# Embedding products between the experts, and expert results added two token tiles at a time

## The reference

```python
x = x + merged @ w_o[i]
x = x + hierarchical_moe(rmsnorm(x, g_ffn[i]), ..., w_exp_gate[i], w_exp_up[i], w_exp_down[i])
ple_gate = jax.nn.sigmoid(rmsnorm(x, g_ple[i]) @ w_ple_gate[i])
x = x + (p[i] @ w_ple[i]) * ple_gate
```

## Time and profile before

| | us |
|---|---|
| three timed runs, median | 2404.42 |
| profiled execution | 2404.93 |
| its span in the trace | 2403.1 |
| TensorE busy in the span | 2284.4 (95%) |
| first add of layer 0 / of layer 1 (start of the embedding block) | 691.18 / 1432.98 |
| half 0 done, ScalarE's table load behind it, layer 0 / layer 1 | 729.56 / 1472.62 |

### The profile page before, as it was taken

The page is one execution under the profiler, slowest core; times in us unless marked ns, Lnnn a source line. Parts: engine busy times, 40 slices in busy tenths (PEclk is TensorE's granted clock), DMA queues, the critical chain, the costliest instruction groups (busy, mean ns, idle before and its releaser), DMA issues. The chain is left out here.

```text
span 2403.1 us, 29859 instructions
## 1 busy us (share of the span) xinstructions
PE 2284.4 (95%) x11904; PEld 1698.6 (71%) x11904; DVE 1003.0 (42%) x1787; ACT 597.2 (25%) x1245; POOL 415.3 (17%) x407
## 2 busy tenths in 40 slices
PE   9989999997899989999998888999989999999998
PEld 7666788654458767788754447877768887888887
DVE  6545533511146454543521136445643435232234
ACT  3523401311134442410311115323540003000012
POOL 2011111122212101111122211111102211111111
PEclk9999999999999999999999999999999999999999
DMA  5114536799962212234899982422213332333321
GB/s 170 46 52 107 134 106 256 319 421 423 420 246 70 62 38 71 58 98 167 327 420 422 422 335 74 108 80 84 81 38 101 91 120 72 103 97 97 97 97 71
DMA packets 291931, 396.57 MB, mean 165 GB/s; under 512 B 32591, under 2 KB 232015, under 8 KB 274379
## 3 DMA queue, kind: packets, MB, share of 16 engines
q1 hardware_dynamic: 274880, 366.27, 42.6%
q0 software_dynamic: 11328, 16.81, 1.9%
q10 hardware_dynamic: 5578, 11.51, 1.8%
HBM read 388.98 MB, written 30.15 MB: 174 GB/s over the span
## 5 line engine op out<-in xcount | busy, mean ns | idle before, releaser
L146 PE MATMUL banks<-h_split,w_high 128*128 128x512 f32 (+1 forms) x2640 | 827.0, 395 | 2.8 <-PEq L3450 1.7
L146 PEld LDWEIGHTS banks<-h_split,w_high 128*128 128x128 f32 x2640 | 482.8, 188 | 104.0 <-issue 8.2
L198 DVE TENSOR_TENSOR w_low<-w_raw,w_high 128x1024 fp32r<-128x1024 f32 (+1 forms) x264 | 321.8, 1220 | 503.3 <-POOL w_high L187 503.1
L187 POOL CAST w_high<-w_raw 128x1024 fp32r<-128x1024 f32 (+1 forms) x264 | 279.1, 1058 | 1434.8 <-PE banks L146 1312.0
L146 PE MATMUL banks<-h_split,w_low 128*128 128x512 f32 (+1 forms) x1320 | 513.5, 389 | 0.0
L146 PEld LDWEIGHTS banks<-h_split,w_low 128*128 128x128 f32 x1320 | 247.8, 188 | 52.4
L146 PE MATMUL banks<-w_high,op_split 128*128 128x512 f32 x736 | 228.5, 390 | 1.4 <-DVE mg_part L1425 1.1
L2159 PE MATMUL banks<-expert_ring,ex_xsT 128*64 128x256 f32 x1408 | 172.5, 401 | 35.2 <-DMA expert_ring<-in_w_exp_up 33.7
L2159 PEld LDWEIGHTS banks<-expert_ring,ex_xsT 128*64 128x64 f32 x1408 | 103.2, 144 | 92.4 <-DMA expert_ring<-in_w_exp_up 37.0
L146 PEld LDWEIGHTS banks<-w_high,op_split 128*128 128x128 f32 x736 | 138.1, 188 | 31.8 <-DVE mg_part L1425 2.4
L146 PE MATMUL banks<-w_low,op_split 128*128 128x512 f32 x368 | 143.2, 389 | 0.0
(11 more groups left out here) (446 smaller groups left out, 2745.6 us busy)
## 6 DMA issues: line engine op xcount, KB each, us to landing
w_raw<-in_w_in SPq DMA_DIRECT2D x142, 512.0 KB, 4.0
expert_ring<-in_w_exp_gate SPq DMA_DIRECT2D x42, 1024.0 KB, 20.6
expert_ring<-in_w_exp_up SPq DMA_DIRECT2D x42, 1024.0 KB, 23.9
expert_ring<-in_w_exp_down SPq DMA_DIRECT2D x42, 1024.0 KB, 23.5
region<-in_w_exp_gate SPq DMA_DIRECT2D x22, 1024.0 KB, 19.9
region<-in_w_exp_up SPq DMA_DIRECT2D x22, 1024.0 KB, 23.3
region<-in_w_exp_down SPq DMA_DIRECT2D x22, 1024.0 KB, 23.6
w_raw<-in_w_gu SPq DMA_DIRECT2D x44, 512.0 KB, 4.0
```

Of the source, the lines that this page charges most:

```text
L146: last = nc.tensor.matmul(out, left, right, start=(start and n == 0), stop=(stop and n == 2), skip_group_check=True)
L187: self.nc.gpsimd.tensor_copy(self.high[:, i % self.SPLIT, 0:n], self.raw[:, i % self.RAW, 0:n]).then_inc(self.high_ready, 1)
L198: self.nc.vector.tensor_tensor(self.low[:, i % self.SPLIT, 0:n], self.raw[:, i % self.RAW, 0:n], self.high[:, i % self.SPLIT, 0:n].bitcast ...
```

## The change

1. The embedding's eight half-tiles are multiplied on TensorE ahead of the experts at positions 16, 17 and 19 to 24 (BETWEEN), into PSUM bank 7, and ScalarE takes each ahead of that expert's silu. w_ple is loaded as one DMA of 1 MB behind the loads of expert 15, when position 11 has finished, into slot 5.
2. The slot of an expert comes from a table. From expert 12 on slot 5 is not used for experts any more, so five slots remain, and near the end three for the last loads.
3. The first four gate pieces wait for position 25 instead of 29. GpSimd and VectorE convert two of them ahead of the border (GATE_EARLY), the third behind it.
4. In the embedding block VectorE adds tiles 0 and 1 and one choice of tile 2, then forms the low parts of the first two tiles, then adds the rest. TensorE first issues 24 matmuls that nobody reads and 5 more behind each of the first three adds, then transposes the first two tiles, multiplies them by the first six chunks of half 0, and does the same for the other two tiles; the last two chunks follow for all four.
5. The norm's gain (norm_g, 4 KB) is loaded from ScalarE's queue instead of SyncE's.

```diff
-            for q in (e.pairs - 2, e.pairs - 1):
-                c = (q + 1) % GATHERS
-                sp.wait_ge(e.turned, 2 * q + 2)
-                sp.dma_start(*embedding.load_pair(c)).then_inc((p_landed0, p_landed1)[c], 16)
-            sp.wait_ge(e.down_done, EXPERTS - 2)
+                if n == SLOT_LEFT + 3:
+                    sp.wait_ge(e.down_done, SLOT_LEFT)
+                    embedding.load_weights(sp)
+            sp.wait_ge(e.down_done, e.order.index(GATE_RAW_AFTER) + 1)
             gate_stream.loads(sp, 0, gate_stream.RAW)
...
-            gate_stream.split_highs(pool, 0, gate_stream.SPLIT)
+            gate_stream.split_highs(pool, 0, GATE_EARLY)
...
+SLOT_OF = (*(n % 6 for n in range(17)), 0, 1, 2, 3, 4, 0, 1, 3, 4, 2, 0, 1, 3, 0, 1)
+SLOT_LEFT = 12
+GATE_RAW_AFTER, GATE_EARLY = 25, 2
-EARLY_PRODUCTS = 4
+BETWEEN = (16, 17, 19, 20, 21, 22, 23, 24)
...
+    def freed(self, sp, done, held):
+        if self.before(held):
+            sp.wait_ge(done, self.order.index(self.before(held)[-1]) + 1 if self.refilled else self.before(held)[-1] + 1)
...
     def tensor(pe):
-        for i in range(EARLY_PRODUCTS, 2 * NT):
-            wait(pe, embedding.ready, i - 1)
-            embedding.product(i, k.ps[:, i % 2, :]).then_inc(multiplied, 1)
-        for t in range(NT):
-            norm.open_tile(pe, t, (results.added, 2 * t + 2))
...
+        early = 2 * st.SPLIT
+        unread(k, 7, 24)
+        for n in (1, 2, 3):
+            pe.wait_ge(results.added, n)
+            unread(k, 7, 5)
+        for pair in range(PAIRS):
+            pe.wait_ge(results.added, 4 * pair + 4)
+            norm.turn_rows(pe, pair, k.x)
+            for c in range(early):
+                norm.pair_split(pe, pair, c)
+                st.rows(pe, c // 2, c % 2, 2, c, lambda t: k.ps[:, t, :], tiles=(2 * pair, 2 * pair + 1))
+        for c in range(early, DC):
+            norm.pair_split(pe, PAIRS - 1, c)
+            st.rows(pe, c // 2, c % 2, 2, c, lambda t: k.ps[:, t, :])
...
-        for t in range(NT):
+        for t in (0, 1):
             results.add(k, dve, gate, t)
+        dve.wait_ge(results.landed[2], 16)
+        results.add_choice(k, dve, gate, 2, 0)
         dve.wait_ge(norm.gain_landed, 16)
-        for step in "h0 h1 h2 h3 h4 w3 h5 h6 h7".split():
-            (norm.low if step[0] == "h" else st.split_low)(dve, int(step[1]))
+        for c in range(DC):
+            norm.low_pair(dve, 0, c)
+            if c == 3:
+                st.split_low(dve, 2)
+        results.add_choice(k, dve, gate, 2, 1)
+        results.add(k, dve, gate, 3)
+        for c in range(DC):
+            norm.low_pair(dve, 1, c)
+        st.split_low(dve, 3)
         norm.following_vector(dve)
```

More of the change, by code:

```diff
@@ L298, in scale @@
         self.nc.scalar.activation(x, x, ACT.Copy, scale=self.ss[:, t:t + 1]).then_inc(done, 1)
+PAIRS, PAIR = NT // 2, 2 * P
 class Norm:
+    places = tuple(tuple((bank + c // 2, c % 2 * PAIR) for c in range(DC)) for bank in (2, 4))
     def __init__(self, k, ctx, tag, gain, banks, xn, follows=False, small=None):
@@ L460, in turn_pair @@
     def turn_pair(self, pe, pair):
-        wait(pe, self.low_done, DC * pair)
         pe.wait_ge(self.xn_dve, pair + 1)
         pe.wait_ge(self.xn_act, pair + 1)
[L465 to L487, removed]
+        self.turn_rows(pe, pair, self.xn)
 class FinalNorm(LateNorm):
-    places = (LateNorm.places[0], tuple((5 + c // 2, c % 2 * PAIR) for c in range(6)) + ((0, PAIR), (1, PAIR)))
+    places = (Norm.places[0], tuple((5 + c // 2, c % 2 * PAIR) for c in range(6)) + ((0, PAIR), (1, PAIR)))
     def __init__(self, k, ctx, tag, gain, xn, junk, stream, closing, gained, g):
@@ L1741, in _ @@
             e.down(pe, 1)
[L1742 to L1745, removed]
-                wait(pe, embedding.ready, i - 1)
-                embedding.product(i, k.ps[:, i % 2, :]).then_inc(multiplied, 1)
+            e.multiply(pe, 2, embedding.product)
         @block.scalar
@@ L1791, in _ @@
             act.preload_act_table_set("silu_and_others")
[L1792 to L1795, removed]
+            e.activate(act, embedding.take)
         @block.vector
@@ L1973, in _ @@
             e.vectors(dve, 2)
-            for i in range(gate_stream.SPLIT):
+            for i in range(GATE_EARLY):
                 gate_stream.split_low(dve, i)
@@ L2061, in held, with slot, before @@
         return self.order[n] if self.order[n] < EXPERTS else RESIDENT
+    def slot(self, held):
+        return SLOT_OF[held] if self.refilled else held % len(self.slots)
+    def before(self, held):
+        return [n for n in range(held) if self.slot(n) == self.slot(held)]
+    def freed(self, sp, done, held):
+        if self.before(held):
+            sp.wait_ge(done, self.order.index(self.before(held)[-1]) + 1 if self.refilled else self.before(held)[-1] + 1)
     def refill(self, pool, out, weights, column, last_row, landed):
@@ L2171, in down @@
     def down(self, pe, n):
[L2172 to L2173 removed]
+        held = self.held(n)
+        u = self.slot(held)
+        pe.wait_ge(self.down_landed[u], 16 * (len(self.before(held)) + 1))
         if self.refilled and self.order[n] == EXPERTS:
@@ L2334, in tensor @@
     def tensor(pe):
-        for i in range(EARLY_PRODUCTS, 2 * NT):
-            wait(pe, embedding.ready, i - 1)
-            embedding.product(i, k.ps[:, i % 2, :]).then_inc(multiplied, 1)
-        for t in range(NT):
-            norm.open_tile(pe, t, (results.added, 2 * t + 2))
-        pe.wait_ge(embedding.ready, 2 * NT)
-        for e in range(pieces - st.SPLIT):
-            half = e // NT
-            for n in (0, 1):
-                c = 2 * (e % NT) + n
-                if half == 0:
-                    norm.turned_split(pe, c)
-                st.rows(pe, e, n, 2, c, lambda t: k.ps[:, half * NT + t, :])
-                if half == 0:
-                    norm.turn_next(pe, c)
+        early = 2 * st.SPLIT
[12 more added lines that the diff above has]
+            st.rows(pe, c // 2, c % 2, 2, c, lambda t: k.ps[:, t, :])
+        for e in range(NT, pieces - st.SPLIT):
+            for n in (0, 1):
+                st.rows(pe, e, n, 2, 2 * (e - NT) + n, lambda t: k.ps[:, NT + t, :])
         first = DC - 2 * st.SPLIT
```

114 lines of the change are left out of this document (70 added, 44 removed).

## The result

The kernel after takes 2411.63 us (median of 7 runs, 2408.85 to 2414.41) against 2403.89 us (7 runs) for the kernel before on the same chip: a ratio of 1.0031, 95% interval 1.0021 to 1.0040. It is slower, by 0.31%. The prediction (2399.6 us, 2394.5 to 2405.5) had the wrong sign, and the time lies outside its range. The profiled execution took 2409.78 us, span 2407.9, so its span is 4.8 us longer than the profiled one of before; by the medians the difference is 7.7 us. The traces can place the 4.8 us only.

A forecast was written before the change was run, and what follows sets the result against it. TensorE, busy 95% of the span, bounds the kernel, with experts paced by loads. Terms -0.1 + 0.3 (up to the first add) - 1.9 - 3.1 (to half 0's end) = -4.8 us, giving 2399.6 us, range 2394.5 to 2405.5.

The forecast's parts named there:

- w_ple among the loads: Expert stage: 1 MB in the saturated stream delays later expert loads, costing 2.1 us in layer 0, 2.5 in layer 1.
- The products: Between the experts: eight half-tiles, 14.3 us, hide in TensorE's 18.3 us of load waits; cost 0.
- the rival of a starved last expert: Expert stage: fewer slots make expert 31's loads land up to 8.5 us late per layer, 2416.6 us; chance 0.12.
- the prediction's sign for this rival: End of the experts: waits of several us for expert 30 or 31 would show starvation.
- The border: Last expert to first add: one cast and one conversion fewer bring the first add 2.2 us forward in each layer.
- the other reading: Conversions ahead of the first add: the 3.01 us one is long by itself, not from GpSimd overlap; gain only 1.2 us.
- To the end of half 0: Embedding block from the first add: takes 36.5 us, 1.9 us less in layer 0 and 3.1 less in layer 1.
- Later loads: Last gate piece and next block's loads issued some 4 us later, covered by conversions and sigmoids: 0, at most some 2 us.
- The clock: TensorE behind its idle at the border: 4 us at half clock, costing 2 us, falls on unread matmuls.
- the sum of -4.8 us: Whole kernel: net change -0.1 + 0.3 - 1.9 - 3.1 us against the profiled execution.

The follow-up runs named there:

- run 7: Kernel after, slot table kept, but w_ple loaded behind expert 31 and all eight half-tiles multiplied behind the last expert: 2434.80 us (one run).
- run 11: Kernel after, w_ple still loaded early, but all eight half-tiles multiplied behind the last expert: 2439.49 us (one run).
- run 9: Kernel after with all gate casts ahead of the next block's, piece 7's low part earlier and the next block's three spread out: 2405.53 us, ratio 1.0006.
- run 12: Kernel before with only the experts' part (early w_ple, slots, products between experts), embedding block as before: 2411.00 us, ratio 1.0036.

## Why the prediction was wrong

**w_ple among the loads** (+2.1 and +2.5): the mechanism held, the size did not: +3.2 and +3.3 (+3.2 and +3.0 by the means over the traces with and without the early load). The term took 1.049 MB at 421 GB/s, and the stream does run at that rate to about 640 us; behind that the rate fell. 640 to 672 us of before, and then of after (columns as in the earlier trace rows):

```profile
640.00:672.00 32.00, 30.50 (x225) 16.83 (x223) 5.55 (x15) 4.37 (x10) 9.05 (x9) 1.00 1.00 402
```

```profile
640.00:672.00 32.00, 30.45 (x225) 16.74 (x223) 5.38 (x14) 4.37 (x10) 9.04 (x9) 1.00 0.98 383
```

Whether that makes up the 0.5 to 0.8 us above 2.5 is not settled: run 7 has the low rate too (385 GB/s) and no delay.

**The products** (0) were hidden: run 11. **The slots**: the rival of a starved last expert did not come; its up load is issued at 659.46 instead of 649.80 and TensorE waits 2.3 us for it; but run 7, with the same table, waits even 2.9 us there and has no delay, so a wait at this place, the prediction's sign for this rival, does not show it.

**The border** (-2.2 each): VectorE's conversions end 2.1 us earlier against the last gate_up, as worked out. But the first add then waits for y_rows to land (2.3 us of idle where it was 1.8), so 1.6 and 1.4 are left. The two conversions took 3.17 us beside GpSimd's casts, more than twice 1.21; this is the overlap that the prediction took from its row, and the 2.1 us agree with it, where the other reading gave 1.2. It is also what the Trainium skill says (GPSIMD Engine Reference, Key points): the two engines share SBUF interfaces, and an instruction with two SBUF inputs contends.

**To the end of half 0** (-1.9 and -3.1): -2.0 and -2.9. The unread matmuls took 10.5 and 11.0 us against 10.9, and TensorE reached the first transposes well behind the fourth add, as the prediction said. That it fits to 0.2 us is in part luck: in the other five traces with 39 unread matmuls these took 9.2 to 12.1 us and this stretch of the table 37.0 to 39.0 us. The shortest (run 7, layer 0) had none of them at 1.2 GHz, the longest (run 9, layer 1) 6.2 us of them.

**Later loads** (0, "the conversions of the last gate pieces and the sigmoids between them cover that") is the step that failed, in its mechanism: +1.7 and +3.4 us, beyond its bound of 2 in all. The loads are 7 us later against the end of half 0, not 4, since piece 0 is free only when the second pair has used it. And there was too little cover: the sum took the end of half 0 as what everything behind follows, and never asked which wait ends last in half 1. The waits of before had the answer, 1.4 us for pg_low in layer 1. VectorE and GpSimd did their work there in a fixed order, with the next block's conversions ahead of the last gate pieces. Run 9 undoes that order alone: half 1 takes 22.5 and 27.6 us, and the time falls by 6.0 us.

**The clock** was worked out at the border only. It also fell behind the new wait: of the 3.4 us of layer 1's half 1, an estimated 1.7 (half the length of the stretch) are its stretch at 1.2 GHz, and the stretch in the next product costs about as much again. Before, the longest wait in layer 1's half 1 is 2.1 us, after it is 3.2. Of all kernels run, before and run 12 have no stretch at 1.2 GHz there or in the next 10 us; the twelve others, which all wait longer there, have one or two. That the wait brings the clock down is argued from this and not shown: no run changed the wait alone.

With the experts' 6.5 and half 1's 5.1, the 7.9 us won at border and half 0 are gone, and the part behind layer 1 adds 2.1. Two of its stretches at 1.2 GHz are new (from 1503.3 and 2035.8), which would make up more than that; the traces of all kernels spread there from 902.5 to 906.0 us, so the cause of the 2.1 stays open. Against the sum of -4.8 us the traces are 9.6 us worse: 5.1 from half 1, 1.9 from w_ple, 1.4 from the border and 2.1 behind layer 1, less 1.0 at the start and between the layers. The other 2.9 us by which the medians lie apart are in no stretch of these two traces.

## What to carry to other kernels

When a step is made to end earlier, read the waits of the stage behind it first, and ask which engine ends last there and where its chain begins; a wait of 1.4 us already there says that the cover is used up. A tile order that halves the work for its start also keeps a shared buffer longer, and everything queued behind that buffer moves with it. 1 MB that entered the saturated stream ahead of its last consumer cost here 3.0 to 3.2 us by the means, where the stream's rate gives 2.5; so bytes have to be counted in full against what is gained by having them early.

## What the runs showed of the hardware

A second MB in the saturated stream of expert loads cost 4.0 and 3.2 us (single traces, which differ by up to 2.6 us in layer 0 and 0.9 in layer 1) where the rate of 422 GB/s gives 2.5. One of VectorE's conversions took 2.03 us beside GpSimd's casts and 1.22 us without them, so the order of both engines' conversions also changes their length. Layer 1, before, with GpSimd casting from 1468.22 on:

```profile
1468.31 2.03 DVE L198 TENSOR_TENSOR pg_low<-expert_ring,pg_high 128x1024 fp32r<-128x1024 f32 x1 [3.01 <-POOL pg_high L187]
```

After, with GpSimd idle until 1469.95:

```profile
1467.64 1.22 DVE L198 TENSOR_TENSOR pg_low<-expert_ring,pg_high 128x1024 fp32r<-128x1024 f32 x1 [1.42 <-POOL pg_high L187]
```
